# Moving gathered expert pairs out of the last search round, one up product behind the gate table, and a third buffer for v

## The chip, the cores and the metric

The kernel runs on one core of one Trainium2 chip. The metric is the device time of one execution in microseconds. Five engines work side by side: PE (matrix products; PEld is its weight load), DVE and ACT (elementwise work), POOL (elementwise work and indirect gathers) and SP, which here does nothing but issue DMAs. Every engine runs its own instructions strictly in the order in which they are written and waits on semaphores where a step needs another engine or a DMA.

## What is computed

Two transformer blocks over 512 tokens of width 1024, in float32. The change lies in the last part of the first block, a product-key mixture of 16,384 single-neuron experts:

```python
q = einsum(h, w_q)                       # 8 heads, two halves of 128
s1, s2 = q1 . keys1, q2 . keys2          # 128 scores a half
v1, i1 = top_k(s1, 16); v2, i2 = top_k(s2, 16)
vals, c = top_k(v1[:, None] + v2[None, :], 16)
expert = e1 * 128 + e2;  gate = softmax(vals)
act = gelu(einsum('td,ted->te', hb, u_tab[expert]))
out = einsum('te,ted->td', gate * act, v_tab[expert])
```

Each token thus uses 8 x 16 = 128 experts. `h` is the normalised input, and `out` is added to the residual stream `x`.

## The kernel before, in words

The tokens stand in four blocks of 128. The kernel computes the experts of the first three blocks (384 tokens, `DT`) densely: all 16,384 experts, in 128 groups of 128, one *up product* (384 tokens against 128 rows of u, 24 matmuls of 128x384) and one *down product* (18 matmuls of 128x512) for each, weighted by a table of gates that is zero where a token doesn't use the expert. The fourth block is computed by gathering: for each of its 128 tokens' choices POOL fetches a row of u and v together (`uv`, 1 MB for 128 tokens). Two gathers are a *pair*, or *tick* `t` = 0 to 63: `pool_gather` issues it, `dve_dots` takes two dot products with h, `act_tick` the gelu and the gate, and `dve_sums` adds two weighted rows of v to the sum. A pair's buffers are free for pair t + 2 once `dve_sums(t)` is done, and POOL waits for that inside `pool_gather(t + 2)`.

To keep float32 accuracy a product is three matmuls of a high and a low part. ACT makes the high part, `act_u_hi` (L1652) or `act_v` (L2314), and then POOL or DVE the low part, `u_lo` (L1658) or `dve_v` (L2319). `ur`, the raw u, has three buffers; `vraw`, the raw v, has two.

Three stages follow one another:

- *Search* (`*_route`): eight rounds c, one head each. DVE finds the top 16, POOL forms candidates (L2034), multiplies one-hots (L2049) and makes the low parts of eight u's, and PE runs the queries of the next round and eight up products. In each round after the first three pairs are worked on. Round 7 has no queries left.
- *Gates* (`*_gates`): 96 steps q of four tokens. DVE and ACT make one-hot tiles, PE multiplies them to gates (L2155), and ACT copies them (L2174) to `stg`, which SP saves to `g_scratch` every eight steps. Behind every fourth q an up product stands (`up_at`, 24 of them), and `tick_at` has four pairs. Five up products (`up_end`) stand behind the table, to number 95. Up products 0 to 95 (`NE`) are saved in memory.
- *Experts* (`*_experts`): for group j, DVE multiplies the activation by the gates read back (`gti`, L2358) and splits it into `awhl` (L2364, L2366), and PE does the down product. Every fourth j has one of the last 32 up products ahead of it. `tick_in` has the last 39 pairs, one every 3.2 groups.

The order on each queue is written by hand. Between gates and experts, ACT has `act_v(0)` and `act_v(1)` behind up product 94 and its own high part of u 97; DVE has v 0, v 1 and the low parts of u 96 and 97, and then the gate work of group 0; SP has the loads of `gti`, two v's, a u, two saved activations, and then, for each remaining up product, a save and the load of the u five further on, which waits for a low part:

```python
def sp_u(e, n):
    if n >= 3: e.wait_ge(*u_low(n - 3).of("lo", n - 3))
    e.dma_start(ur[:, n % 3, :], a["peer_u"][turn[n]])...
def sp_v(e, j):
    if j >= 2: e.wait_ge(*DN[2].of("v", j - 2))
    e.dma_start(vraw[:, j % 2, :], a["peer_v"][:, j, :])...
```

`act_v(j)` and the last step of the gate work of j wait for down product j - 3, since `vhl` and `awhl` have three buffers.

## Time and profile before

| | |
|---|---|
| median of 3 runs | 2930.76 us (2924.13 to 2932.87) |
| the profiled execution | 2931.42 us, its span 2929.7 us |
| PE busy | 2767.1 us, 94% |
| PE weight loads | 2347.6 us, 80% |
| DVE busy | 1886.2 us, 64% |
| ACT busy | 1191.8 us, 41% |
| POOL busy | 533.2 us, 18% |
| DMA, mean | 171 GB/s over the span |
| chain that ended last | PE 66%, DVE 16%, DMA 9%, ACT 5% |

The shares are means over all stages. Search runs from about 937 to 1333 us, gates to 1541, and experts from 1574 to 2250. "Idle before" in a row is how long that engine had stood still when the instruction began, and the name behind the arrow is what ended the wait. A granted clock of 1.00 is PE's higher level, 2.4 GHz, and 0.50 the lower, 1.2 GHz.

### The profile page before, as it was taken

To read this page: it belongs to the slowest core of one execution; us is meant where nothing else is said; L and a number is where in the kernel's file an instruction comes from. 1 tells how busy PE (TensorE), PEld (TensorE's weight loads), DVE (VectorE), ACT (ScalarE), POOL (GpSimd) and SP (SyncE) were. 2 spreads that over 40 slices of the span, in tenths; PEclk is the share of its full clock that TensorE was granted. 3 is DMA by queue.
4 is the path that set the end of the run, shared out by engine and by line. 5 is a ranking of instruction groups with operands and counts; after the bars stand their busy time and mean duration, and the time that the engine had idled before them with its cause. 6 is when DMAs were issued, how large, how long until landed. Compare 5 with 4: busy or idle time off the path is not lost.

```text
span 2929.7 us, 36988 instructions
## 1 busy us (share of the span) xinstructions
PE 2767.1 (94%) x14045; PEld 2347.6 (80%) x14045; DVE 1886.2 (64%) x3534; ACT 1191.8 (41%) x1928; POOL 533.2 (18%) x393
## 2 busy tenths in 40 slices
PE   8999999989998999989998999999999978999997
PEld 6777878888777999988997888888887556788876
DVE  3334665755555787877975888888886574444434
ACT  5545243233223445447993232323234444322322
POOL 0112220220000778771001111111110011000000
PEclk9999999999999999999999999999999989999999
DMA  4112101003653578775768888888884101222220
GB/s 159 51 51 87 58 29 44 30 30 138 218 207 130 209 285 299 264 268 199 289 231 286 333 318 304 327 323 299 321 307 153 42 29 38 74 99 99 86 101 29
DMA packets 141360, 501.19 MB, mean 171 GB/s; under 512 B 13401, under 2 KB 67073, under 8 KB 111617
## 3 DMA queue, kind: packets, MB, share of 16 engines
q1 hardware_dynamic: 122752, 364.60, 35.1%
q0 software_dynamic: 18432, 134.23, 11.7%
q8 instruction: 113, 1.85, 0.3%
q14 instruction: 63, 0.51, 0.1%
HBM read 450.53 MB, written 48.25 MB: 170 GB/s over the span
## 4 chain that ended last, share of the span: by engine, by line
PE 66%; DVE 16%; DMA 9%; ACT 5%; issue 3%; POOL 1%; SPq 0%; DVEq 0%; ACTq 0%; POOLq 0%
PE bank L244 17%; PE bank L246 17%; PE bank L245 17%; DMA vraw<-in_peer_v_dram 6%; DVE vhl L2319 2%; PE bank L2155 2%; DVE xn L1532 2%; PE bank L2737 1%; PE bank L1117 1%; PE bank L1107 1%; PE bank L740 1%; PE bank L1123 1%; DMA w_raw<-in_w_in_dram 1%; DVE gs L1726 1%; DVE M L2940 1%
## 5 line engine op out<-in xcount | busy, mean ns | idle before, releaser
L244 PE MATMUL bank<-HH,uhl 128*128 128x384 f32 x1024 | 350.4, 342 | 9.1 <-POOL uhl L1658 9.1
L246 PE MATMUL bank<-HH,uhl 128*128 128x384 f32 x1024 | 347.0, 339 | 0.0
L245 PE MATMUL bank<-HL,uhl 128*128 128x384 f32 x1024 | 347.0, 339 | 0.0
L244 PE MATMUL bank<-vhl,awhl 128*128 128x512 f32 x768 | 300.9, 392 | 23.4 <-DVE awhl L2366 22.4
L246 PE MATMUL bank<-vhl,awhl 128*128 128x512 f32 x768 | 299.8, 390 | 0.0
L245 PE MATMUL bank<-vhl,awhl 128*128 128x512 f32 x768 | 299.8, 390 | 0.0
L1715 POOL DMA_INDIRECT gs<-in_uv_dram,idx x128 | 149.5, 1168 | 814.1 <-DVE x L1740 506.0
L2314 ACT ACTIVATE vhl<-vraw 128x1024 fp32r<-128x1024 f32 x128 | 135.6, 1060 | 378.5 <-DMA vraw<-in_peer_v_dram 325.7
L2319 DVE TENSOR_TENSOR vhl<-vraw,vhl 128x1024 fp32r<-128x1024 f32 x128 | 156.3, 1222 | 109.3 <-ACT vhl L2314 109.2
L1658 POOL TENSOR_TENSOR uhl<-ur,uhl 128x1024 fp32r<-128x1024 f32 x69 | 167.5, 2436 | 319.2 <-ACT uhl L1652 318.9
L244 PE MATMUL bank<-HH,whl 128*128 128x512 f32 x528 | 217.4, 412 | 4.7 <-DVE whl L240 3.5
L240 DVE TENSOR_TENSOR whl<-w_raw,whl 128x2048 fp32r<-128x2048 f32 x49 | 113.6, 2318 | 160.2 <-ACT whl L234 160.2
L245 PE MATMUL bank<-HL,whl 128*128 128x512 f32 x528 | 210.8, 399 | 0.0
L246 PE MATMUL bank<-HH,whl 128*128 128x512 f32 x528 | 210.5, 399 | 0.0
L244 PEld LDWEIGHTS bank<-HH,uhl 128*128 128x128 f32 x1024 | 194.0, 189 | 11.7 <-ACT uhl L1652 6.8
L245 PEld LDWEIGHTS bank<-HL,uhl 128*128 128x128 f32 x1024 | 194.3, 190 | 1.7
L246 PEld LDWEIGHTS bank<-HH,uhl 128*128 128x128 f32 x1024 | 194.0, 189 | 0.0
L244 PEld LDWEIGHTS bank<-vhl,awhl 128*128 128x128 f32 x768 | 144.6, 188 | 57.3 <-issue 14.5
L240 DVE TENSOR_TENSOR wfhl<-wf_raw,wfhl 128x2048 fp32r<-128x2048 f32 x37 | 84.8, 2292 | 155.0 <-ACT wfhl L234 155.0
L246 PEld LDWEIGHTS bank<-vhl,awhl 128*128 128x128 f32 x768 | 144.6, 188 | 30.4
L245 PEld LDWEIGHTS bank<-vhl,awhl 128*128 128x128 f32 x768 | 144.6, 188 | 28.6
L1652 ACT ACTIVATE uhl<-ur 128x1024 fp32r<-128x1024 f32 x128 | 134.5, 1052 | 19.4 <-DMA ur<-in_peer_u_dram 19.4
(421 smaller groups left out, 6212.1 us busy)
## 6 DMA issues: line engine op xcount, KB each, us to landing
ur<-in_peer_u_dram SPq DMA_DIRECT2D x128, 512.0 KB, 5.0
vraw<-in_peer_v_dram SPq DMA_DIRECT2D x128, 512.0 KB, 5.4
w_raw<-in_w_in_dram SPq DMA_DIRECT2D x36, 1024.0 KB, 5.0
xn<-in_ada_rows_dram SPq DMA_DIRECT2D x48, 512.0 KB, 4.6
g_scratch<-stg SPq DMA_DIRECT2D x12, 2048.0 KB, 8.4
gti<-g_scratch SPq DMA_DIRECT2D x16, 1536.0 KB, 10.9
wf_raw<-in_f_w_in_dram SPq DMA_DIRECT2D x22, 1024.0 KB, 4.8
act_scratch<-ag SPq DMA_DIRECT2D x96, 192.0 KB, 2.9
```

The costliest lines, as they stand in the source:

```text
L240: e.tensor_tensor(lo, W.tile(k), r32(hi), ALU.subtract).then_inc(*W.low(k).up(k))
L244: e.matmul(out, l[0], r[0], start=start, stop=False)
L245: e.matmul(out, l[0], r[1], start=False, stop=False)
L246: return e.matmul(out, l[1], r[0], start=False, stop=stop)
L740: i = e.matmul(b[:, (j - s) * P:wid[s]], const("tri_ge") if j == s else ones, L[:, off[j]:off[j] + wid[j]], start=j == s, stop=j == NT - 1 ...
L1532: e.scalar_tensor_tensor(out=xn2[:, m % 3, :], in0=xn2[:, m % 3, :], scalar=1.0, in1=cond, op0=ALU.mult, op1=ALU.mult, accum_out=modT[:, m ...
L1652: e.activation(uhl[n % 3][:, 0, :], ur[:, n % 3, :], ACT.Copy).then_inc(*A.up("hi", n))
L1658: e.tensor_tensor(uhl[n % 3][:, 1, :], ur[:, n % 3, :], r32(uhl[n % 3][:, 0, :]), ALU.subtract).then_inc(*u_low(n).up("lo", n))
L1715: e.indirect_dma_start(gs[:, n % 4, :], None, a["uv"], bass.IndirectOffsetOnAxis(ap=idx[:, n:n + 1], axis=0)).then_inc(*gs_land[n % 4].up(n))
L2155: n = e.matmul(b[:, blk(i)], HA[q % NA][:, i, :], HO[q % NA][:, i, :], start=True, stop=True)
L2314: e.activation(vhl[j % 3][:, 0, :], vraw[:, j % 2, :], ACT.Copy).then_inc(*A.up("v", j))
L2319: e.tensor_tensor(vhl[j % 3][:, 1, :], vraw[:, j % 2, :], r32(vhl[j % 3][:, 0, :]), ALU.subtract).then_inc(*V.up("v", j))
```

## The change

1. Round 7 of the search has no pairs: neither gathers, dots, ticks nor sums are left in it, but for the sums of pair 17, which round 6 began. Search now does pairs 0 to 17, gates 18 to 21, and experts 22 to 63 (42, one every 2.9 groups).
2. `up_at` has 23 up products and `up_end` six, 90 to 95. The high parts of u 96 to 98 and the low parts of 96 and 97 go from the end of the gates stage into the first experts.
3. SP loads the activation of group 1 ahead of a u, and v 2 ahead of the activation of group 2. DVE does v 0 and the gate work of group 0 first, and v 1 after that.
4. `vraw` has three buffers, and `sp_v` runs three groups ahead. `gg16`, `dot` and `ga` take the place of three constants that are no longer used.

```diff
-    def act_up(e, R, n):
+    def act_up(e, R, n, ahead=True):
...
-        act_u_hi(e, n + 3)
+        if ahead:
+            act_u_hi(e, n + 3)
...
-    gg16 = new.sb("gg16", [P, P])
-    dot = new.sb("dot", [P, P])
-    ga = new.sb("ga", [P, P])
+    gg16, dot, ga = (const(n) for n in ("m8", "m16", "m32"))
...
-    T3 = 25
+    TD, T3 = 18, 22
...
         dve_dots(e, t)
-        if t:
+        if t > TD:
             dve_sums(e, t - 1)
...
-            if c:
+            if 0 < c < 7:
                 act_tick(e, 3 * c - 3)
...
-        act_tick(e, 20)
...
-            if c >= 2:
+            if 2 <= c < 7:
                 pool_gather(e, 3 * c - 2)
...
-            if c:
+            if 0 < c < 7:
                 pool_gather(e, 3 * c - 1)
...
-    up_at = {4 * i + 2: D2 + i for i in range(24)}
+    up_at = {4 * i + 2: D2 + i for i in range(23)}
     up_end = range(D2 + len(up_at), NE)
-    tick_at = {5 + 23 * i: 21 + i for i in range(T3 - 21)}
+    tick_at = {5 + 23 * i: TD + i for i in range(T3 - TD)}
...
         for n in up_end:
-            act_up(e, R6, n)
+            act_up(e, R6, n, n + 3 < NE)
             if n == NE - 2:
                 all_done(e, *GT)
                 act_v(e, 0)
...
-        u_lo(e, up_end[0] + 1)
         for n in up_end:
-            if n == NE - 2:
-                dve_sums(e, T3 - 1)
-                all_done(e, *GT)
-                dve_v(e, 0)
-                dve_v(e, 1)
-            u_lo(e, n + 2)
+            if n + 2 < NE:
+                u_lo(e, n + 2)
+        dve_sums(e, T3 - 1)
+        all_done(e, *GT)
+        dve_v(e, 0)
...
         sp_v(e, 1)
+        sp_act(e, 1)
         sp_u(e, up_end[0] + 5)
-        sp_act(e, 1)
+        sp_v(e, 2)
         sp_act(e, 2)
...
-        vraw = new.sb("vraw", [P, 2, D])
+        vraw = new.sb("vraw", [P, 3, D])
...
-    tick_in = {1 + 16 * i // 5: T3 + i for i in range(NB - T3)}
+    tick_in = {1 + 29 * i // 10: T3 + i for i in range(NB - T3)}
...
-            if j >= 2:
-                e.wait_ge(*DN[2].of("v", j - 2))
-            e.dma_start(vraw[:, j % 2, :], a["peer_v"][:, j, :]).then_inc(*v_l[j % 2].up(j))
+            if j >= 3:
+                e.wait_ge(*DN[2].of("v", j - 3))
+            e.dma_start(vraw[:, j % 3, :], a["peer_v"][:, j, :]).then_inc(*v_l[j % 3].up(j))
...
         e.activation(x1[:, 3, :], sump, ACT.Copy).then_inc(*GA[1].up("back"))
+        act_u_hi(e, NE)
+        act_u_hi(e, NE + 1)
         for j in range(P):
             if j >= 2:
                 act_v(e, j)
+            if j == 2:
+                act_u_hi(e, NE + 2)
...
         for j in range(P):
-            if j >= 2:
+            if j == 1:
+                u_lo(e, NE)
+            if j:
                 dve_v(e, j)
+            if j == 2:
+                u_lo(e, NE + 1)
...
-            sp_v(e, j + 2)
+            sp_v(e, j + 3)
```

The same `if 0 < c < 7` stands in place of `if c` at the other ticks, dots, sums and the third gather of the round.

### How the order moves

POOL in the last search round, from its candidates on, before (`gs` is a gathered pair, `uhl` the low part of a u, the last two `TENSOR_TENSOR eT` and `oh` the one-hot multiplies):

```order
L2034 TENSOR_TENSOR eT<-v_183 128x1024
L1715 DMA gs<-in_uv_dram,idx 128x2048 x2
L1658 TENSOR_TENSOR uhl_126<-ur,uhl_126 128x1024
L1658 TENSOR_TENSOR uhl_124<-ur,uhl_124 128x1024
L1715 DMA gs<-in_uv_dram,idx 128x2048 x2
L1658 TENSOR_TENSOR uhl_125<-ur,uhl_125 128x1024
L2049 TENSOR_TENSOR eT<-eT,if_186 128x1024
L1658 TENSOR_TENSOR uhl_126<-ur,uhl_126 128x1024
L2049 TENSOR_TENSOR oh<-oh,if_186 128x1024
L1658 TENSOR_TENSOR uhl_124<-ur,uhl_124 128x1024
L1715 DMA gs<-in_uv_dram,idx 128x2048 x2
L1658 TENSOR_TENSOR uhl_125<-ur,uhl_125 128x1024
```

and now:

```order
L2033 TENSOR_TENSOR eT<-v_180 128x1024
L1658 TENSOR_TENSOR uhl_126<-ur,uhl_126 128x1024
L1658 TENSOR_TENSOR uhl_124<-ur,uhl_124 128x1024
L1658 TENSOR_TENSOR uhl_125<-ur,uhl_125 128x1024
L2048 TENSOR_TENSOR eT<-eT,if_183 128x1024
L1658 TENSOR_TENSOR uhl_126<-ur,uhl_126 128x1024
L2048 TENSOR_TENSOR oh<-oh,if_183 128x1024
L1658 TENSOR_TENSOR uhl_124<-ur,uhl_124 128x1024
L1658 TENSOR_TENSOR uhl_125<-ur,uhl_125 128x1024
```

The three pairs have gone; the rest stands as it stood.

SP's queue from the load of the gate table on, before (`agd` is a saved activation, `ag` one that is being saved):

```order
L2259 DMA gti<-g_scratch 128x12x256
L2267 DMA vraw<-in_peer_v_dram 128x1024 x2
L1644 DMA ur<-in_peer_u_dram 128x1024
L2274 DMA agd_232<-act_scratch 128x384
L2274 DMA agd_233<-act_scratch 128x384
L1687 DMA act_scratch<-ag_130 128x384
```

and now:

```order
L2257 DMA gti<-g_scratch 128x12x256
L2265 DMA vraw<-in_peer_v_dram 128x1024 x2
L2272 DMA agd_230<-act_scratch 128x384
L1644 DMA ur<-in_peer_u_dram 128x1024
L2265 DMA vraw<-in_peer_v_dram 128x1024
L2272 DMA agd_231<-act_scratch 128x384
L1688 DMA act_scratch<-ag_129 128x384
```

The u is number 96 before and number 95 now: u 95 used to be loaded ahead of the table. Behind this piece stand, as before, save and u load in turn, and the last of these u's, 100, is still ahead of the next v.

DVE from the last sums of the gates stage to the gate work of group 1, before:

```order
L1740 SCALAR_TENSOR_TENSOR bank<-gs_123,ga_158,bank 128x1024 x2
L2319 TENSOR_TENSOR vhl0_224<-vraw_223,vhl0_224 128x1024
L2319 TENSOR_TENSOR vhl1_225<-vraw_223,vhl1_225 128x1024
L1658 TENSOR_TENSOR uhl0_124<-ur_127,uhl0_124 128x1024
L1658 TENSOR_TENSOR uhl1_125<-ur_127,uhl1_125 128x1024
L2358 TENSOR_TENSOR agd0_231<-agd0_231,gti_227 128x384
L2364 CAST awhl0_228<-agd0_231 128x384
L2366 TENSOR_TENSOR awhl0_228<-agd0_231,awhl0_228 128x384
L2358 TENSOR_TENSOR agd1_232<-agd1_232,gti_227 128x384
```

and now, to v 2:

```order
L1739 SCALAR_TENSOR_TENSOR bank<-gs_123,cst_1,bank 128x1024 x2
L2317 TENSOR_TENSOR vhl0_222<-vraw_221,vhl0_222 128x1024
L2364 TENSOR_TENSOR agd0_229<-agd0_229,gti_225 128x384
L2370 CAST awhl0_226<-agd0_229 128x384
L2372 TENSOR_TENSOR awhl0_226<-agd0_229,awhl0_226 128x384
L1658 TENSOR_TENSOR uhl0_124<-ur_127,uhl0_124 128x1024
L2317 TENSOR_TENSOR vhl1_223<-vraw_221,vhl1_223 128x1024
L2364 TENSOR_TENSOR agd1_230<-agd1_230,gti_225 128x384
L2370 CAST awhl1_227<-agd1_230 128x384
L2372 TENSOR_TENSOR awhl1_227<-agd1_230,awhl1_227 128x384
L1725 SCALAR_TENSOR_TENSOR gs_123,cst_1<-gs_123,h2r_153 128x1024 x2
L2317 TENSOR_TENSOR vhl2_224<-vraw_221,vhl2_224 128x1024
```

Group 0 is complete after one v, and the low parts of u 96 and 97 have moved behind the gate work of groups 0 and 1; that of 97 is the next row.

## Rows read from the trace of the kernel before

**Rows 1.** Windows: last search round; experts (busy of each engine, clock, DMA share, GB/s)

```profile
1259.00:1333.00 74.00, 64.92 (x346) 63.86 (x345) 45.41 (x134) 30.99 (x68) 52.52 (x27) 0.93 0.74 261
1574.00:2210.00 636.00, 627.54 (x2905) 537.57 (x2906) 527.66 (x747) 192.38 (x295) 92.11 (x76) 1.00 0.86 316
```

**Rows 2.** PE's timeline, last search round (start, us, instruction [idle before <-releaser])

```profile
1273.60 0.41 PE L244 MATMUL bank<-HH,uhl 128*128 128x384 f32 x1 [1.87 <-POOL uhl L1658]
...
1300.66 0.41 PE L244 MATMUL bank<-HH,uhl 128*128 128x384 f32 x1 [4.35 <-POOL uhl L1658]
...
1318.00 0.41 PE L244 MATMUL bank<-HH,uhl 128*128 128x384 f32 x1 [2.85 <-POOL uhl L1658]
```

**Rows 3.** Windows around two pauses of PE

```profile
1298.00:1308.00 10.00, 7.33 (x33) 7.37 (x34) 3.20 (x7) 4.26 (x8) 9.98 (x6) 0.83 0.88 313
...
1564.00:1578.00 14.00, 3.77 (x9) 3.02 (x10) 9.69 (x14) 5.75 (x8) 3.14 (x2) 0.51 0.52 185
```

**Rows 4.** POOL's timeline, last search round

```profile
1295.12 1.77 POOL L1715 DMA_INDIRECT gs<-in_uv_dram,idx  x1 [5.13 <-DVE cf L2001]
...
1300.49 2.36 POOL L2049 TENSOR_TENSOR eT<-eT,if 128x1024 f32<-128x1024 f32 x1
...
1313.27 0.97 POOL L1715 DMA_INDIRECT gs<-in_uv_dram,idx  x1 [3.33 <-DVE bank L1740]
```

**Rows 5.** DVE's timeline, last search round

```profile
1291.72 2.63 DVE L1740 SCALAR_TENSOR_TENSOR bank<-gs,ga,bank 128x1024 f32<-128x1024 f32 x2
```

**Rows 6.** SP's timeline, its DMA issues between gates and experts

```profile
1549.87 0.38 SPq L2259 DMA_DIRECT2D gti<-g_scratch  x1
...
1552.17 1.64 SPq L1644 DMA_DIRECT2D ur<-in_peer_u_dram  x1
...
1572.66 0.33 SPq L1644 DMA_DIRECT2D ur<-in_peer_u_dram  x1
```

**Rows 7.** ACT's timeline between gates and experts

```profile
1538.47 0.49 ACT L1681 ACTIVATE ag<-bank 128x384 f32<-128x384 f32 x1 [1.77 <-PE bank L246]
...
1539.80 1.13 ACT L2174 ACTIVATE stg<-bank 128x512 f32<-128x512 f32 x1
1543.53 0.49 ACT L1681 ACTIVATE ag<-bank 128x384 f32<-128x384 f32 x1 [2.60 <-PE bank L246]
...
1547.68 0.49 ACT L1681 ACTIVATE ag<-bank 128x384 f32<-128x384 f32 x1 [2.72 <-PE bank L246]
...
1563.13 1.06 ACT L1652 ACTIVATE uhl<-ur 128x1024 fp32r<-128x1024 f32 x1 [10.79 <-DMA ur<-in_peer_u_dram]
...
1570.04 1.01 ACT L2325 ACTIVATE x<-bank 128x1024 f32<-128x1024 f32 x1
```

**Rows 8.** DVE's timeline between gates and experts

```profile
1570.28 2.36 DVE L1658 TENSOR_TENSOR uhl<-ur,uhl 128x1024 fp32r<-128x1024 f32 x2
1572.55 0.55 DVE L2358 TENSOR_TENSOR agd<-agd,gti 128x384 f32<-128x384 f32 x1
```

**Rows 9.** PE's timeline in the experts' stage

```profile
1574.23 0.77 PE L244 MATMUL bank<-vhl,awhl 128*128 128x512 f32 x1 [14.16 <-DVE awhl L2366]
...
1584.36 0.39 PE L244 MATMUL bank<-vhl,awhl 128*128 128x512 f32 x1
...
1600.70 0.34 PE L244 MATMUL bank<-HH,uhl 128*128 128x384 f32 x1
...
1818.28 0.47 PE L244 MATMUL bank<-vhl,awhl 128*128 128x512 f32 x1 [2.18 <-DVE awhl L2366]
```

**Rows 10.** PE's waits behind the gates (total us, times, longest)

```profile
PE bank L244 <- DVE awhl L2366: 22.4, 11, 14.2
```

**Rows 11.** The v buffer: landing times of its 128 loads

```profile
DMA to landing us min/median/max: 3.4/5.4/15.5
```

**Rows 12.** Two windows of 40 us in the experts' stage

```profile
1610.00:1650.00 40.00, 40.00 (x189) 34.55 (x188) 32.58 (x50) 11.12 (x20) 5.93 (x5) 1.00 0.94 354
...
1730.00:1770.00 40.00, 40.00 (x188) 34.26 (x187) 32.62 (x48) 12.51 (x18) 4.91 (x4) 1.00 0.86 306
```

More of the change, by code:

```diff
@@ L1989, in dve_route @@
                 dve_sums(e, 3 * c - 4)
+            if 0 < c < 7:
+                dve_dots(e, 3 * c - 3)
             if c:
-                dve_dots(e, 3 * c - 3)
                 e.wait_ge(*A.of("gexp", c - 1))
@@ L1994, in dve_route @@
             dve_top16(e, V, NT, cand, cand2, vv, ii, "c", c)
-            if c:
+            if 0 < c < 7:
                 dve_sums(e, 3 * c - 3)
@@ L2004, in dve_route @@
                 e.tensor_tensor(oh4[i], by16(cf[:, i, :, :]), iota16, ALU.is_equal).then_inc(*V.up("oh", c, i))
-            if c:
+            if 0 < c < 7:
                 dve_dots(e, 3 * c - 2)
@@ L2017, in dve_route @@
             e.tensor_copy(idx[:, s16], idxf[:, :]).then_inc(*V.up("idx", c))
-            if c:
+            if 0 < c < 7:
                 dve_sums(e, 3 * c - 2)
@@ L2042, in pool_route @@
             lo(4)
-            if c:
+            if 0 < c < 7:
                 pool_gather(e, 3 * c - 1)
@@ L2051, in pool_route @@
                 lo(6 + i)
-            if c:
+            if 0 < c < 7:
                 pool_gather(e, 3 * c)
@@ L2240, in build @@
     R7x = Ring(banks[6:8] + banks[0:6])
-    v_l = [new.lands("v_land") for _ in range(2)]
+    v_l = [new.lands("v_land") for _ in range(3)]
     g_land = [new.lands("g_land") for _ in range(2)]
@@ L2310, in act_v @@
         T, A, V, G = DN
-        e.wait_ge(*v_l[j % 2].of(j))
+        e.wait_ge(*v_l[j % 3].of(j))
         if j >= 3:
             e.wait_ge(*T.of("d", j - 3))
-        e.activation(vhl[j % 3][:, 0, :], vraw[:, j % 2, :], ACT.Copy).then_inc(*A.up("v", j))
+        e.activation(vhl[j % 3][:, 0, :], vraw[:, j % 3, :], ACT.Copy).then_inc(*A.up("v", j))
     def dve_v(e, j):
@@ L2318, in dve_v @@
         e.wait_ge(*A.of("v", j))
-        e.tensor_tensor(vhl[j % 3][:, 1, :], vraw[:, j % 2, :], r32(vhl[j % 3][:, 0, :]),
+        e.tensor_tensor(vhl[j % 3][:, 1, :], vraw[:, j % 3, :], r32(vhl[j % 3][:, 0, :]),
                         ALU.subtract).then_inc(*V.up("v", j))
```

## The prediction

> **What bounds the kernel now.** I read the page's slices first: PE is busy for nine tenths nearly everywhere, so time is won only where PE stands still. Then the table of windows: in the last search round and behind it PE is busy for 64.9 of 74 us, in the experts' stage for 627.5 of 636 [rows 1]. PE's timeline names the pauses the change speaks of. The last search round has three, each ended by POOL's low part of a u: 1.87, 4.35 and 2.85 us [rows 2]. After such a pause the granted clock is low: the 10 us around the second have a mean of 0.83 [rows 3], so a sixth of 10 us, 1.7 us, goes on top of each. Between gates and experts PE idles for 14.16 us until expert 0's gate-weighted activation is ready, and the 14 us from 1564 have 0.51, close to the lower level of 1.2 GHz [rows 3, 9]; the first down product after it runs from 1574.23 to about 1580.2 where later ones take 4.08, 1.9 us lost. In the experts' stage 11 waits for the same tile sum to 22.4 us; without the 14.16 that leaves 8.2 us in ten waits [rows 10]. What is late there is v: ACT waited for its load, which takes 5.4 us as the median and 15.5 at the worst [rows 11], and only two buffers hold it.
>
> All times below are on the clock of the profiled run (2931.42 us, span 2929.7); the median of the runs shown, 2930.76, is 0.7 below it, and the forecast is set against the median.
>
> **Last round without pairs.** The round's three ticks (three pairs of gathers on POOL, six dot products and six sums on DVE) are dropped there and appear later. The second and third pause are made by POOL standing in a gather: it waits 5.13 us for DVE's sum, issues two gathers, and only then comes the u part that PE needs; again 3.33 us before the third [rows 4]. DVE's sum of 2.63 us lies ahead of the round's one-hot rows [rows 5], so these come 5 us earlier too (2.4 of dots, 2.6 of sums). Without the gathers the u part of product 61 follows its high part, near 1292, and PE wants it at 1296.3; that of 62 has its multiply ahead (2.36 us [rows 4], about 1291.6 to 1294.0) and is done by 1296.5 against 1300.4. Each is early by 2 us or more. So 4.35 + 2.85 + 2 x 1.7 = **10.6 us** go. The first pause, 1.87 us, lies behind the gather of the round before, which stays. Bounds: 0 (were the multiplies the cause) and 11.
>
> **Six products behind the table.** ACT was free at 1536.70 (1538.47 less 1.77) but copied the last gate tile at 1539.80, behind the gelu and the high part of up product 90 [rows 7]. With that product moved behind, the copy ends 3.1 us earlier, at 1537.8, and the table's save and its load back, which begins at 1549.87 [rows 6], move to 1546.7. PE's work does not change; five of the six products end at 1555.9 (1560.07, where PE now stops, less one product of 4.15 [rows 7]). What is new: the load of u 95 used to leave before the table's last save; now it stands on SP's queue behind the table's load, two v's and an activation. The u that stood there before was used 13.3 us after the table's load was issued (1549.87 to 1563.13 [rows 6, 7]); one 0.19 MB load more adds 0.5. So u 95 is there at 1560.5, its high part at 1561.6, its low part (1.18 us, half of the pair in [rows 8]) at 1562.8. PE idles for 6.9 us, then runs product 95 at the lower clock, to 1562.8 + 4.15 + 1.9 = 1568.9. The gate work of expert 0 needs 1.54 us (1572.55 to its end before PE's start [rows 8, 9]) and now has v 0 alone ahead of it, not two v's and two u's; DVE ends it near 1567.7, hidden. Down product 0 starts at 1569.3, when ACT has emptied the bank: 4.9 us sooner than 1574.23, 6.8 with its clock.
>
> **The parts ordered by need, and what is late next.** The high parts of u 96 and 97 now stand behind product 95's gelu and the copy of x (1.01 us [rows 7]): 96 at 1571.3. DVE then: low part 96, 1572.5; v 1, 1573.7; weights 1, 1575.2; two dots, 2.4 us, 1577.6; v 2, 1578.8; low part 97, 1580.0. PE gets through down 0 (1573.4), up 96 (1577.6), down 1 (1581.7) and, its weights ready at 1581.5, down 2 (1585.8). But SP holds the load of u 100 until low part 97 frees its buffer, and v 3 and v 4 are queued behind it, as v 2 and v 3 are now behind the one of 1572.66 [rows 6]. The moved low part holds that queue for 7.4 us longer. v 3 is issued at 1580.4, lands 5.4 us later [rows 11], 1585.8, and 1.06 (high), 1.18 (low), 1.18 (low part 98) and 1.54 put weights 3 at 1590.7. PE waits 4.9 us and loses 1.7 to the clock; down 3 ends at 1596.5. Dots and sums (5.0), v 4 and weights 4 end at 1598.4, so down 4 at 1602.5, where it ended at 1600.70 [rows 9]. The whole handover is thus **2 us worse**, not better: the first product is early and the fourth is late. Bounds: 14.16 + 1.9 = 16 better (no wait at all), 6 worse (v 3 lands at the 11 us that a load behind the table's takes).
>
> The Trainium skill, DMA: Bandwidth & Descriptors, section on the anatomy of one DMA, fits a transfer at 2.0 us plus its bytes over 436 GB/s. It gives 3.2 us for a v and 1.2 for the u ahead of it, 4.4 us for v 3 where I take the median of 5.4, and the handover would be 1 us better by it; the fit is for the other path of issue, so the row is taken.
>
> **Third buffer for v.** A load is now issued at the same moment for one expert further on, 5.1 us more of slack (four experts in 1584.36 to 1600.70 [rows 9], 4.08 us each, and one up product of 4.15 per four). The longest of the ten waits is 2.18 us [rows 9], well inside it; the denser gathers may make a few new ones. I take 7 of the 8.2 us as gone; bounds 8.2 gained and, were they doubled, 8.2 lost.
>
> **Three ticks more in the experts' stage** (42 for 39, one per 2.9 experts for 3.2). DVE: 3 x 5.0 = 15 us on 527.7 busy of 636 [rows 1], 85%: covered, since PE stays the longer. Between dots and sums of a pair and the next the distance shrinks by 0.3 of an expert; gathers have some 19 us. If the cover goes, each tick costs PE up to 5 us. DMA: per expert 0.524 (v) + 0.131 (u) + 0.147 (activation) + 0.197 (table) + 2.097/3.2 MB = 1.65 MB becomes 1.72; at PE's 5.12 us that is 336 GB/s after 323. The best 40 us moved 354 at a share of 0.94, 377 at a full one [rows 12], so 336 is a share of 0.89. Nothing is charged. Moving gg16, dot and ga into unused constants costs nothing; that only makes room.
>
> Sum: -10.6 + 2 - 7 = **-15.6 us**; 2930.8 becomes **2915**.
>
> **The rivals.**
> - *v stays late* (0.14). The added 2.6% of traffic eats the third buffer. For it: the stage already moves 316 GB/s at 0.86 [rows 1], and gathers, table and u's come in bursts. The ten waits stay or double: 2931 - 10.6 + 2 = 2922 to 2930. The Trainium skill, DMA: Bandwidth & Descriptors, Specifications, puts the memory side at about 358 GB/s per core. By that 336 is 94% of the limit, not 89%, and the row of 354 agrees with it; without it this rival would have 0.10.
> - *The handover works* (0.11). u 95 lands with the table, or v 3 comes in 4 us: half of the 16 us, 2907.
> - *Round 7 keeps its pauses* (0.07), the multiplies on POOL being the cause: the change would not do there what it says. 2930.8 + 2 - 7 - 3 = 2923.
> - *DMA becomes the bound* (0.06), the slower side. The experts' stage, 662 us now, then lasts 128 x 1.72 MB over what the queues sustain. It loses as much as round 7 wins (8.6 net) at 329 GB/s; at 320, about what the stage moves now, it takes 689 us, 27 more, 2949; at 306, a 40 us stretch of now [rows 12], 2981. Against it: now nothing but v waits, and stretches of 354 exist.
>
> **How the numbers follow.** The forecast has 0.62 with its own range of 2909 to 2921. A measurement tells 0.3%, 8.8 us, from no change: faster is below 2922, and holds the forecast, the good handover and half of the second and fourth case, 0.79; slower is the DMA bound, 0.06; the rest 0.15. The range of 2906 to 2926 leaves out the DMA bound, the best handover and the worst of the late v's.
>
> **What would show it.** Right: in the last round one POOL-ended PE pause of about 1.9 us and none of 3 or 4; the last table save some 3 us earlier against the start of the gates; a PE pause of 6 to 7 us before up product 95, one of about 5 before down 3 with SP's v loads issued right behind a u; one to three short waits for awhl later; DVE at 85%, DMA near 335 GB/s. Wrong: pauses of 3 us left in the last round; no pause before down 3; ten or more waits for awhl, or experts further apart than 5.2 us with DMA at its ceiling.

## Result and the profile after

The changed kernel takes **2909.46 us** (median of 5 runs, 2904.7 to 2912.65) where the kernel before takes 2928.12 us beside it on the same chip (5 runs, 2924.13 to 2932.87). The ratio is 0.9931 with a 95% interval of 0.9919 to 0.9943: 20 us faster by the ratio, 18.7 by the two medians, where 15.6 were forecast. The profiled execution took 2909.46 us with a span of 2907.7, so spans can be compared: 2929.7 has become 2907.7. One run of this study, of the kernel r7_gathers_later below, took 3011.77 us at a mean clock of 0.891 where every other has 0.978 or more, and is left out of its median. The page of the changed kernel, busy time of each engine and then the chain that ended last:

```profile
PE 2759.3 (95%) x14045; PEld 2343.5 (81%) x14045; DVE 1890.3 (65%) x3534; ACT 1195.7 (41%) x1928; POOL 536.7 (18%) x393
...
PE 80%; DVE 9%; ACT 5%; DMA 3%; issue 2%; POOL 1%; SPq 0%; DVEq 0%; ACTq 0%; POOLq 0%
```

The work is the same (DVE 1886.2 us before, 1890.3 now); the share of PE in the chain went from 66% to 80%, and that of DVE and DMA from 25% to 12%.

To see where the 22 us of span went, I cut both traces at four matmuls that both kernels have. They are the first up product behind the last scores of the search, the first gate product, up product 97 (it stands behind down product 4, so it closes the handover), and up product 127, the last. Kernel before, PE's timeline, at three of the marks (up product 97 is the row of 1600.70 in [rows 9]):

```profile
1254.83 0.42 PE L244 MATMUL bank<-HH,uhl 128*128 128x384 f32 x1
...
1337.61 0.55 PE L2155 MATMUL bank<-HO,HA 128*128 128x128 f32 x1 [4.33 <-ACT HO L2142]
...
2229.40 0.34 PE L244 MATMUL bank<-HH,uhl 128*128 128x384 f32 x1
```

Changed kernel, PE's timeline: the same four marks, and between them every pause of PE from the last round on, but for the twelve of 0.8 to 1.4 us inside the gates stage that both kernels have (start, us, instruction, [idle before <- releaser]):

```profile
1253.55 0.42 PE L244 MATMUL bank<-HH,uhl 128*128 128x384 f32 x1
...
1272.32 0.41 PE L244 MATMUL bank<-HH,uhl 128*128 128x384 f32 x1 [1.88 <-POOL uhl L1658]
...
1325.23 0.55 PE L2154 MATMUL bank<-HO,HA 128*128 128x128 f32 x1 [4.34 <-ACT HO L2141]
...
1551.08 0.66 PE L244 MATMUL bank<-HH,uhl 128*128 128x384 f32 x1 [7.09 <-DVE uhl L1658]
...
1558.68 0.47 PE L244 MATMUL bank<-vhl,awhl 128*128 128x512 f32 x1 [0.95 <-ACT ag L1681]
...
1578.62 0.47 PE L244 MATMUL bank<-vhl,awhl 128*128 128x512 f32 x1 [3.16 <-DVE awhl L2372]
...
1586.15 0.47 PE L244 MATMUL bank<-vhl,awhl 128*128 128x512 f32 x1 [1.58 <-DVE awhl L2372]
...
1590.36 0.34 PE L244 MATMUL bank<-HH,uhl 128*128 128x384 f32 x1
...
2207.76 0.34 PE L244 MATMUL bank<-HH,uhl 128*128 128x384 f32 x1
```

The differences of these rows give the parts (us), against the terms of the forecast:

| part | before | after | moved | forecast |
|---|---|---|---|---|
| up to the first mark | 1254.8 | 1253.6 | -1.3 | 0 |
| last search round | 82.8 | 71.7 | -11.1 | -10.6 |
| gates and handover | 263.1 | 265.1 | +2.0 | +2 |
| experts, up product 97 to 127 | 628.7 | 617.4 | -11.3 | -7 |
| the rest | 700.3 | 699.9 | -0.4 | 0 |

The first and the last part run the same work in both kernels. Over all fourteen kernels of this study the first lies between 1252.3 and 1257.9 and the last between 695.7 and 700.6, so the 1.7 us there are scatter. The two middle parts scatter too. With the same instructions on PE and no pairs in it, the last round takes 70.1 to 72.5 us over nine kernels. Gates and handover in the order of before take 263.1 to 265.6 over the seven kernels that have it. The +2.0 of that part is therefore not told apart from scatter, though what makes it up can be read: PE's pauses there sum to 23.3 us for 24.7, and the rest, PE's own time, is 241.8 for 238.4 (238.3 to 239.0 in all seven with the old order, 242.0 in the other kernel with the new one).

The 11 waits for `awhl` have become two, both in the handover. Waits of the changed kernel's PE behind the gates (total, times, longest), in place of [rows 10]:

```profile
PE bank L244 <- DVE uhl L1658: 7.1, 1, 7.1
PE bank L244 <- DVE awhl L2372: 4.7, 2, 3.2
```

Who waited for the v buffer's loads, before and then after (ACT's idle time, times):

```profile
  ACT vhl L2314: 325.7, 81
```

```profile
  ACT vhl L2312: 34.4, 7
DMA to landing us min/median/max: 3.4/5.9/14.6
```

The loads land no sooner than in [rows 11], they are issued sooner. And the middle 580 us of the experts' stage, before and then after (PE, PEld, DVE, ACT, POOL busy, PE clock, DMA share, GB/s):

```profile
1610.00:2190.00 580.00, 571.77 (x2653) 489.52 (x2652) 482.17 (x684) 175.06 (x270) 82.88 (x69) 1.00 0.86 317
```

```profile
1610.00:2190.00 580.00, 580.00 (x2709) 500.74 (x2708) 509.79 (x713) 185.02 (x285) 93.25 (x74) 1.00 0.88 330
```

PE no longer stands still at all. DVE is at 88% and the queues at 0.88.

### The profile page after: what moved, and what is told of

Same layout as the page of the kernel before. It is cut to its first block, busy times and chain, and to the rows that moved or that the text cites. A ratio compares the mean times of both kernels' runs of the same rounds, so it can differ in the third digit from the quotient of the medians.

```text
span 2907.7 us, 36988 instructions
## 1 busy us (share of the span) xinstructions
PE 2759.3 (95%) x14045; PEld 2343.5 (81%) x14045; DVE 1890.3 (65%) x3534; ACT 1195.7 (41%) x1928; POOL 536.7 (18%) x393
## 4 chain that ended last, share of the span: by engine, by line
PE 80%; DVE 9%; ACT 5%; DMA 3%; issue 2%; POOL 1%; SPq 0%; DVEq 0%; ACTq 0%; POOLq 0%
PE bank L244 21%; PE bank L246 21%; PE bank L245 21%; PE bank L2154 2%; DVE xn L1532 1%; PE bank L2743 1%; PE bank L1107 1%; PE bank L740 1%; PE bank L1117 1%; PE bank L1123 1%; DMA w_raw<-in_w_in_dram 1%; DVE M L2946 1%; DVE m L2942 1%; PE bank L346 1%; DVE whl L240 1%
## 5 line engine op out<-in xcount | busy, mean ns | idle before, releaser
L244 PEld LDWEIGHTS bank<-HH,uhl 128*128 128x128 f32 x1024 | 194.0, 189 | 11.1 <-ACT ag L1681 7.4
```

The lines of the kernel that those rows point to most:

```text
L244: e.matmul(out, l[0], r[0], start=start, stop=False)
```

## The experiments

All were measured beside the kernel before, in three groups: r7_only to after_two_v beside a median of 2930.05 us, u95_ahead to r7_gathers_later beside 2929.89, the rest beside 2927.84. The changed kernel stands in none of them, so kernels of different groups are compared by their ratios. The columns of the parts use the four marks above, in one profiled execution of each.

| kernel | median us | ratio to before, 95% | last round | gates, handover | experts |
|---|---|---|---|---|---|
| before | 2928 to 2930 | 1 | 82.8 | 263.1 | 628.7 |
| changed | 2909.46 | 0.9931 (0.9919 to 0.9943) | 71.7 | 265.1 | 617.4 |
| r7_only | 2947.89 | 1.0063 (1.0047 to 1.0078) | 72.0 | 263.4 | 657.8 |
| v3_only | 2917.36 | 0.9960 (0.9947 to 0.9973) | 82.8 | 263.4 | 617.4 |
| after_old_handover | 2907.07 | 0.9924 (0.9911 to 0.9937) | 70.4 | 263.5 | 617.4 |
| after_two_v | 2948.78 | 1.0067 (1.0052 to 1.0082) | 70.4 | 265.8 | 660.0 |
| u95_ahead | 2903.31 | 0.9924 (0.9905 to 0.9943) | 71.7 | 260.5 | 617.4 |
| v3_ahead | 2901.82 | 0.9921 (0.9903 to 0.9940) | 70.1 | 260.3 | 617.4 |
| both_ahead | 2897.55 | 0.9903 (0.9884 to 0.9921) | 72.5 | 255.9 | 617.4 |
| r7_gathers_later | 2921.75 | 0.9981 (0.9970 to 0.9992) | 78.4 | 265.6 | 629.6 |
| r7_thin_dve | 2920.64 | 0.9972 (0.9959 to 0.9985) | 75.3 | 263.6 | 628.7 |
| r7_only_thin_dve | 2914.88 | 0.9950 (0.9932 to 0.9967) | 71.7 | 264.3 | 622.5 |
| saves_ahead | 2894.94 | 0.9882 (0.9864 to 0.9899) | 70.4 | 249.9 | 617.4 |
| saves_and_gather18 | 2897.66 | 0.9885 (0.9867 to 0.9903) | 72.3 | 252.8 | 617.4 |

### The parts of the change alone

**r7_only**: the kernel before with the last round emptied and its pairs moved, and nothing else.

```diff
-            if c:
+            if 0 < c < 7:
...
-    tick_in = {1 + 16 * i // 5: T3 + i for i in range(NB - T3)}
+    tick_in = {1 + 29 * i // 10: T3 + i for i in range(NB - T3)}
```

> The kernel before, with the last search round alone emptied of pairs (pairs 18 to 21 in the gates stage, 22 to 63 in the experts' stage, one every 2.9 groups), two v buffers and the old handover. My theory, by parts that add: 11 us less than before (2917 against 2928), PE with one POOL-ended pause of 1.9 us in the last round, the ten or so short waits for awhl still there (sum 8 us or a little more). Rival 1, the new spacing of the pairs and not the third buffer removed those waits: 2907, no waits. Rival 2, denser pairs without the third buffer make v later still: waits of 16 us or more in sum, 2922 to 2926.

The round gains its 10.8 us, as forecast. Yet the kernel is *slower* than before by 0.63%, outside all three cases that I had written down: the experts' stage loses 29. PE's waits for `awhl` behind the gates in this kernel:

```profile
PE bank L244 <- DVE awhl L2366: 43.5, 29, 14.0
```

They come in clusters, and the trace shows where one begins. SP's queue, then ACT and DVE of the same stretch:

```profile
1697.24 0.33 SPq L2267 DMA_DIRECT2D vraw<-in_peer_v_dram  x1
1698.77 0.33 SPq L2274 DMA_DIRECT2D agd<-act_scratch  x1
1699.14 0.43 SPq L2259 DMA_DIRECT2D gti<-g_scratch  x1
1702.90 0.33 SPq L2267 DMA_DIRECT2D vraw<-in_peer_v_dram  x1
```

```profile
1717.37 1.06 ACT L2314 ACTIVATE vhl<-vraw 128x1024 fp32r<-128x1024 f32 x1 [8.79 <-DMA vraw<-in_peer_v_dram]
1718.46 1.23 DVE L2319 TENSOR_TENSOR vhl<-vraw,vhl 128x1024 fp32r<-128x1024 f32 x1 [7.97 <-ACT vhl L2314]
```

The v issued at 1702.90, next behind a load of the gate table (1.5 MB, one every eight groups), is there only at 1717.37: 14.5 us, where the median load of this kernel takes 5.6. Two buffers are two groups of cover, 2 x 5.14 = 10.3 us, less what ACT and DVE need. The v is late, DVE stands for 8 us, and then has the sums and dots of a pair to catch up with. It is no single case: in this kernel the 17 v loads that are issued within 6 us behind a table load take 10.5 us at the median, the other 111 take 5.3. In the kernel before it is 10.3 and 4.9, so the loads are late in both. No run moves or splits the table's load, so this link is read from the traces and not tested.

**v3_only**: the third buffer alone.

```diff
-        vraw = new.sb("vraw", [P, 2, D])
+        vraw = new.sb("vraw", [P, 3, D])
...
-            sp_v(e, j + 2)
+            sp_v(e, j + 3)
```

> The kernel before, with a third buffer for v alone (and gg16, dot and ga in the unused constants), the third load issued right behind the last up load. My theory: 11 us less than before, 2917, no waits for awhl in the experts' stage behind the first one of 14 us, the three pauses in the last search round as before. Rival: the waits come from the traffic of gathers, table and u's, and a buffer only moves them: within 3 us of before.

All waits of the stage are gone, and it takes 617.4 us, the same as in every kernel with three buffers: this is PE's own time. (The old pause of 14 us before down product 0 is still there, 14.5.) The buffer alone is worth 11.3 us there, with the old spacing of the pairs.

**after_old_handover**: r7_only and the third buffer, that is, the changed kernel with the order of before between gates and experts.

> Both of these, so the changed kernel but for the handover: 24 up products in the gates stage, five behind, and the old order of first experts' parts. My theory, that the new handover costs 2 us: 2928 - 22 = 2906, 2 to 3 us below the changed kernel, PE's pause before down product 0 14 us as before, none after it. Rival: the new handover is worth some 5 us, since down product 0 starts sooner: 2914 or more.

The ratios 0.9924 and 0.9931 have intervals that overlap, so the two aren't told apart. Gates and handover take 263.5 us for 265.1, within the scatter of that part. The new order of the handover brings nothing by itself; that it costs 2 us fits these numbers and is not shown by them. The rival, that it is worth 5 us, falls.

**after_two_v**: the changed kernel with two buffers; v 2 is loaded ahead of the u's 99 and 100.

> The changed kernel with two v buffers (v 2 loaded once v 0's low part is done, ahead of the loads of u 99 and u 100; a third buffer is not there for v 2 to be loaded early). My theory: the waits for awhl come back, 9 to 12 us above the changed kernel's 2909, 2919 to 2921. Rival, the spacing of pairs did it: 2909 to 2911.

The miss is large: 39 us, not 9 to 12. The stage takes 660.0 us, with these waits of PE (two of them, 4.8 us, lie ahead of the stage, in the handover):

```profile
PE bank L244 <- DVE awhl L2375: 35.4, 28, 3.3
```

So the third buffer is worth 11 us at one pair per 3.2 groups and 40 to 43 us at one per 2.9. It is what lets the pairs leave the search.

### Is it DVE's time or the gathers' traffic?

**r7_only_thin_dve**: r7_only, where the dots and sums of pairs 22 to 63 work on 64 of 1024 columns; gathers and v loads are whole. (The output thus lacks most of the fourth block's experts.)

```diff
+            w = 64 if t >= T3 else D
...
-            e.scalar_tensor_tensor(out=u, in0=u, scalar=1.0, in1=h, op0=ALU.mult, op1=ALU.mult,
+            e.scalar_tensor_tensor(out=u[:, 0:w], in0=u[:, 0:w], scalar=1.0, in1=h[:, 0:w], op0=ALU.mult, op1=ALU.mult,
```

> The kernel with the last round emptied and two v buffers (2948), with the dots and sums of pairs 22 to 63 over 64 of 1024 columns: most of the fourth block's result is left out, every gather is still made in full. Theory, the time that DVE spends between a v's low part and the next, on top of a load that can't be issued before it, makes the waits for awhl: they go, 2908 to 2916. Rival, the gathers' traffic makes v's loads late: within 5 us of 2948.

The same 580 us of r7_only, then of this kernel:

```profile
1610.00:2190.00 580.00, 552.69 (x2541) 468.51 (x2540) 472.89 (x665) 169.54 (x270) 88.59 (x72) 1.00 0.84 312
```

```profile
1610.00:2190.00 580.00, 579.76 (x2705) 499.76 (x2704) 359.88 (x718) 181.79 (x285) 86.72 (x74) 1.00 0.90 330
```

With the same gathers, more traffic per second (330 GB/s for 312) and two buffers, PE stands still for 0.24 us; what the stage still loses to 617.4 lies mostly ahead of them, in a wait of 2.78 us at 1595. Traffic alone therefore doesn't make the waits. A v behind the table's load is late; whether PE feels it depends on how soon DVE is through with what has piled up. Less work on DVE or a third buffer each take nearly all the waits away. How long the v loads took in this kernel its trace does not say.

### The last round

**r7_gathers_later**: the kernel before, with the gathers of pairs 20 and 21 each behind the low part that PE waits for.

```diff
-            if c:
+            if 0 < c < 7:
                 pool_gather(e, 3 * c - 1)
...
+                if c == 7 and not i:
+                    pool_gather(e, 3 * c - 1)
-            if c:
+            if 0 < c < 7:
                 pool_gather(e, 3 * c)
...
+            if c == 7:
+                pool_gather(e, 3 * c)
```

> The kernel before, all pairs where they were, but in the last search round the second pair's gathers stand behind the low part of product 62 and the third's behind that of product 64. My theory, that PE's second and third pause are POOL standing in a gather: both go though DVE does all its dots and sums there, 8 to 11 us less than before, 2917 to 2920. Rival, the one-hot multiplies or DVE's load are the cause: one or both pauses of 3 to 4 us stay, at most 4 us less.

Only 4.3 of the 11 us come, and not from shorter waits. POOL no longer stands in a gather ahead of those low parts, yet PE waits as long as before, in more and shorter pauses. PE's waits in the window from 1265 to 1340, before and then here (total, times, longest):

```profile
PE bank L244 <- POOL uhl L1658: 9.1, 3, 4.4
```

```profile
PE bank L244 <- POOL uhl L1658: 9.2, 5, 2.7
```

What has fallen is PE's working time, with the clock. The last round, before and then here (PE, PEld, DVE, ACT, POOL busy, PE clock, DMA share, GB/s):

```profile
1254.83:1337.61 82.78, 69.37 (x372) 68.10 (x371) 48.45 (x146) 38.73 (x89) 56.69 (x29) 0.93 0.74 262
```

```profile
1257.94:1336.38 78.44, 64.85 (x373) 63.16 (x371) 50.70 (x146) 39.22 (x89) 56.80 (x29) 0.99 0.77 276
```

The work is 4.5 us shorter at a mean clock of 0.99 for 0.93: none of the five pauses, of 1.4 to 2.7 us, was followed by the lower clock. Some 1.6 us of this lie behind the first pause, ahead of everything that was moved: the up product there took 4.2 us for 5.8. By the whole times the kernel gains 5.6 us (2 to 9); the profiled execution, 2933.93 us, is the longest of the nine, 12 above their median, so only its last round is read here. What POOL waits for instead, in the same kernel:

```profile
1299.33 3.26 POOL L2049 TENSOR_TENSOR eT<-eT,if 128x1024 f32<-128x1024 f32 x1 [3.84 <-DVE eT L2004]
```

The one-hot multiply stands 3.84 us for DVE, which has the dots and sums of the pairs ahead of the row that it needs.

**r7_thin_dve**: the kernel before, with the dots and sums of pairs 18 to 20 over 64 columns, nothing moved. (The output lacks most of those pairs.)

> The kernel before with the dots and sums of pairs 18 to 20, those of the last search round, taken over 64 of 1024 columns: part of the fourth token block's result is left out, all gathers, ticks and waits stay. If DVE's time in the round, which delays both the one-hots and the release of the gathers, is what holds POOL: both later pauses of PE go or fall under 1 us, 9 to 11 us less than before, 2918 to 2921. If it is the place of the gathers on POOL's queue and their issue: a pause of 2 to 4 us stays, at most 6 us less.

It gives 7.5 of the 11 us (82.8 to 75.3), and here the waits do shrink. Pauses of 0.17, 0.32, 0.34 and 1.51 us are left behind the first, 2.3 us in sum where there were 7.2. So most of what the round lost was DVE's time, on which POOL waited. The rest may be POOL's own issue of gathers, which no run takes alone. In the nine kernels whose last round has no pairs, with round 6 untouched, both later pauses are gone.

### The handover

The next kernels are the changed kernel with another order of SP's queue alone. **u95_ahead** issues the load of u 95 ahead of the wait for the table's last save, as before the change:

```diff
+        sp_u(e, up_end[0] + 5)
...
-        sp_u(e, up_end[0] + 5)
```

> The changed kernel with one line moved: the load of u 95 goes ahead of the load of the gate table, not behind it. My theory, that the new pause of 7.1 us before up product 95 is this load's place on SP's queue: the pause is gone, the table lands 1.3 us later, PE then waits about 2 us before down product 0, and the later wait before down 3 stays at 3 to 5 us; in all 5 to 7 us less than the changed kernel, 2902 to 2905 against 2909.5. Rival, PE is held by the table itself: the pause only moves to down product 0, within 2 us of the changed kernel.

The pause of 7.09 us before up product 95 is gone, and one before down product 0 has come:

```profile
1554.38 0.77 PE L244 MATMUL bank<-vhl,awhl 128*128 128x512 f32 x1 [5.14 <-DVE awhl L2372]
```

I expected about 2 us there. The later wait, 3.16 us, now stands before down product 4. The part is 4.6 us shorter. The whole times don't show a gain of that size: the ratio is 0.9924 for 0.9931, with intervals that overlap, and the same holds for v3_ahead (0.9921). Both gains are read from one trace each, in a part that scatters by up to 2.5 us with the same instructions.

**v3_ahead** issues v 3 ahead of u 99 and v 4 ahead of u 100, whose buffers wait for a low part:

```diff
+        for n, j in ((NE - 2, 3), (NE - 1, 4)):
+            sp_save(e, n)
+            sp_v(e, j)
+            sp_u(e, n + 5)
```

> The changed kernel with v 3 issued ahead of the load of u 99 and v 4 ahead of that of u 100. My theory, that v 3 is late because it is queued behind the load of u 100, which waits for a low part: the wait before down 3 (3.2 us) is gone, one of 1.5 to 2.5 us before down 4 stays (two dots and two sums on DVE), 3 to 4.5 us less than the changed kernel: 2905 to 2906.5. Rival, DVE is late by itself: the wait before down 3 stays, no difference.

The wait before down product 3 is gone, one of 1.96 us before down product 4 is left, inside the expected 1.5 to 2.5, and the part is 4.8 us shorter. It was SP's queue, not DVE's work, that made v 3 late.

**both_ahead** has both edits.

> Both moves. My theory: they add, 10 to 12 us less than the changed kernel, 2897.5 to 2900. Rival, they mend the same delay twice: as the better of the two alone.

They add up: 9.2 us in this part, just under the 10 to 12 expected. What is left is one pause of 5.67 us before down product 0, and ACT's timeline names it:

```profile
1552.72 0.49 ACT L1681 ACTIVATE ag<-bank 128x384 f32<-128x384 f32 x1 [9.01 <-DMA act_scratch<-ag]
```

The gelu of product 94 waits 9 us for the buffer of product 91's activation, whose save stands on SP behind the table load, which waits for the table's save. **saves_ahead** therefore issues the save of product 91 ahead of the table load and that of product 92 behind the first two v's. Against both_ahead:

```diff
+        sp_save(e, up_end[1])
...
+        sp_save(e, up_end[2])
...
-        for n in up_end[1:-2]:
-            sp_up(e, n)
+        sp_u(e, up_end[1] + 5)
+        sp_u(e, up_end[2] + 5)
+        sp_up(e, up_end[3])
```

> The kernel with u 95, v 3 and v 4 ahead (2897.5), with the save of up product 91 also ahead of the table's load and that of 92 behind the first two v's. In its trace ACT waits 9.0 us for a buffer whose save lands behind the table. Theory: that wait goes, down product 0 starts some 4.5 us sooner and with the clock not fallen, 4 to 6.5 us less, 2891 to 2893.5. Rival, v 0's landing is just as late: within 2 us.

This is the kernel with the lowest median of the study, 2894.94 us: 1.2% below the kernel before. Its interval lies clear of the changed kernel's, but overlaps with that of both_ahead; the median is 2.6 us below that kernel's, for the 4 to 6.5 expected. In the trace the pause is gone, as the theory has it. Gates and handover take 249.9 us, 6.0 less than in both_ahead and 15.2 less than in the changed kernel, and these are PE's pauses left there behind the gates:

```profile
1548.63 0.47 PE L244 MATMUL bank<-vhl,awhl 128*128 128x512 f32 x1 [0.95 <-ACT ag L1681]
...
1571.79 0.47 PE L244 MATMUL bank<-vhl,awhl 128*128 128x512 f32 x1 [2.30 <-DVE awhl L2379]
```

**saves_and_gather18** also moves the gathers of pair 18, in round 6, behind a low part, against the 1.88 us pause.

> The same, with the gathers of pair 18 in round 6 behind the low part of product 56. Theory: PE's pause of 1.9 us at the start of round 7 goes with its 1.7 us of lower clock, 3 to 4 us less than the kernel with the saves ahead. Rival, as the move of gathers within the full last round (7 of 11 us, with new pauses) suggests, POOL is late elsewhere: no gain.

That pause goes, and one of 2.09 us comes 15 us later, as the rival has it. No gain: 0.9885 for 0.9882. Part of the gain that I had put down wasn't there to be had, since in saves_ahead the 1.9 us pause is followed by a clock of 1.00.

## Why the prediction was right, and where a step was not

**Sign and size.** 15.6 us forecast, 20 measured, and the two parts that are clear of scatter went the way they were put. Of the 4.8 us between forecast and sum of the parts (20.4), 4.3 are one term.

**The mis-sized term: "I take 7 of the 8.2 us as gone."** It was 11.3. The step summed the idle fields of ten waits, and these understate the loss. Four groups and an up product take PE 20.58 us undisturbed (617.4 over 30 such steps). The one step of the kernel before that holds the waits of 2.18 us [rows 9] and 0.63 us takes 1831.53 - 1807.61 = 23.92: 3.34 lost for 2.81 shown. Its two ends in PE's timeline:

```profile
1807.61 0.34 PE L244 MATMUL bank<-HH,uhl 128*128 128x384 f32 x1
...
1831.53 0.34 PE L244 MATMUL bank<-HH,uhl 128*128 128x384 f32 x1
```

Over all ten, 11.3 for 8.2, so some 0.3 a wait; in r7_only 40.4 for 29.5. The idle field runs from the modelled end of a pipelined matmul: in the down products undisturbed matmuls start 0.23 us apart and are shown 0.39 long, and the first behind a pause is followed after 0.31. That makes some 0.25 a wait that no idle field shows, and starts are the better measure. None of the one to three short waits that I had left for the changed kernel came.

**"Three ticks more ... Nothing is charged."** Right for the changed kernel, for a reason that the step left out. It put DVE at 85% as covered "since PE stays the longer". A mean share doesn't say that: r7_only has the same work on DVE, and the stage loses 29 us against the kernel before. The cover is the third buffer, and the two terms that I priced apart, 0 and -7, are one. For the change without the buffer my working gives -10.6 + 2 = -8.6 us; after_two_v measured a ratio of 1.0067, some 20 us slower than before. The worst landing of 15.5 us [rows 11] against two buffers' 10.3 us was a sign that waits would come; the step used it for nothing. It doesn't give their sum, which rose with the pairs for each group while the worst landing stayed (15.1 in r7_only).

**Last round, -10.6.** 11.1 measured, and one pause of 1.88 us left, as said. The two terms came as they were put: the two pauses of 7.2 us are gone, and PE's own time in the round fell by 3.9 (69.4 to 65.5) for the 3.4 of the clock. The reason given was too narrow. With "POOL standing in a gather" removed alone, PE waits 9.2 us for 9.1, and all that is gained, 4.3 us, is clock; with DVE's time for the same pairs removed, 4.9 of the 7.2 us of waiting go, and 7.5 us in all. I had both in the argument ("these come 5 us earlier too") but put the weight on the first. The rival that the round keeps its pauses was wrong for this change. For a change that would only have moved the gathers it comes near: the waits stay, the multiply on POOL among them, though it stands for DVE.

**Handover, +2.** Measured +2.0, within the scatter of that part, so the close match is partly luck. The steps can still be followed one by one. The gates now start 12.4 us earlier (1337.61 and 1325.23), so 12.4 is added to times of the changed kernel. SP's timeline there:

```profile
1534.03 0.38 SPq L2257 DMA_DIRECT2D gti<-g_scratch  x1
...
1568.62 0.33 SPq L1644 DMA_DIRECT2D ur<-in_peer_u_dram  x1
1568.99 0.91 SPq L2265 DMA_DIRECT2D vraw<-in_peer_v_dram  x2
```

and ACT's high part of v 3:

```profile
1573.50 1.06 ACT L2312 ACTIVATE vhl<-vraw 128x1024 fp32r<-128x1024 f32 x1 [6.43 <-DMA vraw<-in_peer_v_dram]
```

| step | forecast | measured + 12.4 |
|---|---|---|
| table's load | 1546.7 | 1546.4 |
| PE pause before up product 95 | 6.9 | 7.09 |
| down product 0 starts | 1569.3 | 1571.1 |
| v 3 is issued | 1580.4 | 1581.4 |
| v 3 lands after | 5.4 | 4.5 |
| PE pause before down product 3 | 4.9 | 3.16 |
| end of down product 4 | 1602.5 | 1602.7 |

Down product 0 started 1.8 us later than put, so PE waited less for v 3, whose load was issued 1.0 us later and took 0.9 less: 1573.50 - 1568.99 = 4.5 us. The errors cancel.

The fit of the Trainium skill (DMA: Bandwidth & Descriptors, the section on the anatomy of one DMA), with the u ahead, gives an estimate of 4.4 us for v 3. The section gives that fit for the other path of issue, and 4.5 us here is one load; still, the trace lies nearer to it than to the median of 5.4 us that I took.

The clock term was right here. After the pause before down product 3 the clock is low, and after the next, of 1.58 us, it is not:

```profile
1578.00:1582.00 4.00, 3.38 (x11) 2.72 (x12) 3.96 (x7) 1.17 (x4) 0.00 (x0) 0.73 1.04 353
...
1586.00:1590.00 4.00, 3.85 (x17) 3.21 (x18) 3.83 (x7) 0.58 (x1) 0.81 (x1) 1.00 1.00 383
```

From down product 3 to 4 are 7.53 us; less the pause of 1.58 and the usual 4.08 that is 1.87 lost for 1.7 put down. What was wrong is the rule behind it, that each pause of 2 to 4 us has its 1.7: the last section has pauses that cost none.

**The rivals.** *v stays late by traffic* falls: no wait is left in the stage, and r7_only_thin_dve makes the same transfers with two buffers and hardly a wait. *DMA becomes the bound* falls: the stage moves 330 GB/s at a share of 0.88, as forecast (336 at 0.89), and PE is never idle. *The handover works* did not come true; v3_ahead and u95_ahead show what it takes, a load that isn't queued behind a blocked one. What I did not see is how much lay there: the bound of 16 us that I gave for that part was nearly within reach, and saves_ahead takes 13.2 of it (263.1 to 249.9).

One chance was added up wrong. "Faster" was given 0.79; the cases that it names, 0.62, 0.11 and half of 0.14 and of 0.07, make 0.84. And the 3 us taken off once more in the price of *Round 7 keeps its pauses* have no source.

## What to carry to other kernels

The median landing doesn't price a buffer. Here two buffers covered 10.3 us and the loads took 5.4 at the median, yet the missing buffer cost 11 us, and 40 when the pairs moved closer by a tenth. The worst landing shows that waits can come and not how many: it was about the same in both. What rose was DVE's work for each group, beside which a late v has to be caught up. Price a moved piece of work and the buffer that hides it as one term, and ask what the sum would be without the buffer.

On a queue that issues in order, a load or a save inherits every wait that stands ahead of it. Five issues (u 95, v 3, v 4 and two saves) put ahead of blocked ones on SP's queue, with no other change in the work, gained 15 us in this part and 14 by the ratios of the whole times. The order by need on the engines had brought none of it.

A part that agrees with its forecast to a tenth of a microsecond, as the +2.0 of the handover does, proves little while the same instructions scatter by 2 us. The pauses and their releasers are the better test.

## What the runs showed of the hardware that I had not expected

The same length of pause did not always cost the clock. Behind the pause of 2.18 us in the experts' stage of the kernel before [rows 9] the granted clock stayed at 1.00, while the one of 1.88 us in the last round of the changed kernel was followed by 10 us at a mean of 0.83. The first window is of the kernel before, the second of the changed one:

```profile
1816.00:1826.00 10.00, 7.82 (x35) 6.45 (x35) 9.69 (x13) 4.35 (x5) 0.78 (x1) 1.00 0.61 197
```

```profile
1272.00:1282.00 10.00, 9.68 (x47) 9.71 (x48) 9.96 (x51) 2.37 (x8) 8.34 (x5) 0.83 0.82 290
```

The same pause in the same place did not always cost it either. In five of the fourteen kernels the pause of 1.9 us at the start of round 7 was followed by the full clock, and the up product behind it took 4.2 us; in the others, but for saves_and_gather18 that hasn't the pause, it took 5.8 or 5.9. The window of after_old_handover, whose last round has the same instructions as that of the changed kernel:

```profile
1272.00:1282.00 10.00, 9.27 (x54) 9.30 (x55) 9.96 (x54) 3.52 (x11) 8.34 (x5) 1.00 0.90 335
```

So 1.6 us of any difference between two executions can be this alone. No run here tells why.

Over stretches of 20 and 30 us the queues moved more than the mean of 330 GB/s. First 20 us of the kernel before, then 30 us of the changed one, around the first down products:

```profile
1625.00:1645.00 20.00, 20.00 (x94) 17.18 (x94) 15.13 (x22) 4.63 (x8) 2.58 (x3) 1.00 1.03 391
```

```profile
1575.00:1605.00 30.00, 25.27 (x109) 20.84 (x108) 28.42 (x40) 9.76 (x15) 4.91 (x4) 0.94 0.97 367
```

The Trainium skill (DMA: Bandwidth & Descriptors, Specifications) puts the memory side at about 358 GB/s per core. These stretches lie above it, at 391 and 367, so by the traces that figure is no ceiling for one core running alone. A share of 1.03 shows that such short windows are rough to some per cent.
